# Sample attention of a decoder trunk step: logits and index scores on four column groups, values of four heads in one product per page

## What is computed

```python
NB, ST, PAST, PAGE = 8, 8, 256, 128       # samples, their new tokens, past positions, page
N_KV, GROUP, HEAD_DIM, N_IDX_HEADS, D_IDX = 2, 4, 64, 4, 64
# scores that choose the positions, for each query token of sample b
dots  = einsum('bqhd,bsd->bqhs', qi, ki_all_of_sample_b)
score = einsum('bqh,bqhs->bqs', wi, relu(dots));   top 66 of the 264 positions
# attention over the chosen positions
logits = einsum('bqngd,bqknd->bqngk', q, ks) * 64**-0.5 + bias
p = softmax(logits);   o = einsum('bqngk,bqknd->bqngd', p, vs)
# then, over all 576 tokens, for three branches A (convolution), C (gating), B (attention)
merged = sig(gA)*(yA @ w_pa) + sig(gB)*(yB @ w_pb) + sig(gC)*(yC @ w_pc)
x = LN(alpha*x + (1+g1)*(merged @ w_o));  then a mixture of 16 experts, top 2 inside one group
```

## Time and profile before

| | |
|---|---|
| median of 3 runs (lowest, highest) | 1200.29 us (1197.52, 1201.43) |
| the profiled execution: its own time, its span in the trace | 1202.89 us, 1200.9 us |
| TensorE matmul busy, weight loads busy | 1047.5 us (87%), 715.6 us (60%) |
| VectorE, ScalarE, GpSimd busy | 473.7 us, 181.4 us, 256.0 us |
| mean granted TensorE clock | 0.925 of full speed |
| DMA | 218.4 MB, mean 182 GB/s |

### The profile page before, as it was taken

The page is one execution under the profiler, slowest core; times in us unless marked ns, Lnnn a source line. Parts: engine busy times, 40 slices in busy tenths (PEclk is TensorE's granted clock), DMA queues, the critical chain, the costliest instruction groups (busy, mean ns, idle before and its releaser), DMA issues. The chain is left out here.

```text
span 1200.9 us, 21915 instructions
## 1 busy us (share of the span) xinstructions
PE 1047.5 (87%) x8902; PEld 715.6 (60%) x8902; DVE 473.7 (39%) x1174; ACT 181.4 (15%) x445; POOL 256.0 (21%) x306
## 2 busy tenths in 40 slices
PE   4699999965999989999999999972999999998940
PEld 3577777533776757777877774552655555554520
DVE  0211999912357888662110302446213211110108
ACT  2200112112221211210111110010111111111102
POOL 1300016375221222222223541000100000000034
PEclk9798999987999999998889999995699999999975
DMA  9923536264615223131017207124296999999954
GB/s 318 306 44 114 145 141 232 88 246 164 209 27 154 58 71 128 36 99 34 10 59 170 106 1 291 70 68 193 72 375 255 406 385 381 384 398 415 360 134 128
DMA packets 93570, 218.40 MB, mean 182 GB/s; under 512 B 23696, under 2 KB 42503, under 8 KB 89373
## 3 DMA queue, kind: packets, MB, share of 16 engines
q1 hardware_dynamic: 71428, 183.83, 42.4%
q0 software_dynamic: 5936, 19.16, 5.1%
q10 hardware_dynamic: 16113, 14.06, 3.9%
HBM read 198.95 MB, written 21.06 MB: 183 GB/s over the span
## 5 line engine op out<-in xcount | busy, mean ns | idle before, releaser
L1604 PE MATMUL bank<-arena 128*128 128x288 f32 (+7 forms) x2288 | 609.4, 424 | 33.2 <-DVEq L1259 14.6
L1604 PEld LDWEIGHTS bank<-arena 128*128 128x128 f32 (+2 forms) x2288 | 430.0, 199 | 196.6 <-issue 100.6
L1926 PE MATMUL bank<-arena 128*32 128x256 f32 x3136 | 182.6, 384 | 11.1 <-issue 8.3
L1926 PEld LDWEIGHTS bank<-arena 128*32 128x32 f32 x3136 | 103.1, 110 | 82.5 <-issue 16.3
L1559 DVE TENSOR_TENSOR arena<-arena,bank 128x128 f32<-128x128 f32 x49 | 14.2, 289 | 245.5 <-ACT arena L1070 245.5
L799 POOL TENSOR_SCALAR arena<-arena 128x288 f32<-128x288 f32 x48 | 45.0, 938 | 234.6 <-ACT arena L1036 234.6
L1947 PE MATMUL bank<-arena 128*32 128x256 f32 x1568 | 94.6, 381 | 0.0
L1608 PE MATMUL bank<-arena 128*128 128x128 f32 (+6 forms) x327 | 50.1, 287 | 41.4 <-DVE arena L1371 14.4
L1141 DVE SCALAR_TENSOR_TENSOR arena<-arena 128x512 f32<-128x512 f32 x120 | 81.9, 742 | 0.0
L1608 PEld LDWEIGHTS bank<-arena 128*128 128x128 f32 (+6 forms) x327 | 37.9, 153 | 57.9 <-issue 21.5
L850 POOL DMA_INDIRECT arena<-h,ints x13 | 13.3, 1025 | 267.9 <-PE bank L1908 225.0
(11 more groups left out here) (254 smaller groups left out, 788.7 us busy)
## 6 DMA issues: line engine op xcount, KB each, us to landing
arena<-in_w_e_gate SPq DMA_DIRECT2D x16, 2048.0 KB, 11.3
arena<-in_w_e_up SPq DMA_DIRECT2D x16, 2048.0 KB, 16.0
arena<-in_w_e_down SPq DMA_DIRECT2D x16, 2048.0 KB, 10.8
arena<-in_w_ada SPq DMA_DIRECT2D x12, 2048.0 KB, 12.7
arena<-in_w_in SPq DMA_DIRECT2D x10, 2048.0 KB, 9.9
expert_rows<-arena POOLq DMA_DIRECT2D x1, 5120.0 KB, 17.3
arena<-in_x_prompt SPq DMA_DIRECT2D x8, 512.0 KB, 5.4
expert_rows<-arena ACTq DMA_DIRECT2D x28, 96.0 KB, 7.2
```

Of the source, the lines that this page charges most:

```text
L1604: last = pe.matmul(out, a, b, start=k == 0, stop=k == len(pairs_) - 1)
L1926: last = pe.matmul(out, HG[:, g % 2, k, a:a + BLK], gate_up[i % 2][:, :, k, c * P:c * P + P], start=k == 0, stop=k == KT - 1)
```

## The change

Four things, with the steps of the plan otherwise in their order:

1. The dots and logits of the samples run on four column groups of TensorE. Group g writes 32 of the 128 output partitions: those of key-value group n = g // 2 and of samples 4z to 4z + 3 with z = g % 2. The queries stand in four zeroed copies; copy x holds sample x and sample 4 + x only. So a step has 4 rounds (x) of 4 matmuls (g) of 32 x 256, each accumulating over x, and 4 matmuls of 32 x 64. In the logits the groups 0 and 1 read SBUF partitions 0 to 63 and the groups 2 and 3 read 64 to 127; in the dots all four read the same 64.
2. All copies (`QIM` and `QM`, six of them) are made once, at `("kit", 0)`; the copies at the logits steps and the zeroing at `("kts", 0)` are gone.
3. The values steps of c = 0, 1, 2 are gone; one step `("pv", "s")` stands where that of c = 3 stood. It has one product of 512 columns for the new positions and 16 products, one for each page, with 64 moving columns: 8 tokens x 2 x 4 heads.
4. The transposed probabilities of all four c are kept in `PS4`, which lies where the key pages were. VectorE's copy at `("pt", "s", c)` no longer waits for a values step. The copies of the result have 256 columns, and `yb_up` reaches 17 in place of 20.

```diff
-        if c < NC - 1:
-            sides[at + 2] += [("pv", "s", c)]
...
-            plan += [("gate", "B", f, h)] + ([("pv", "s", NC - 1)] if (f, h) == (0, 0) else []) + [("proj", "B", f, h)]
+            plan += [("gate", "B", f, h)] + ([("pv", "s")] if (f, h) == (0, 0) else []) + [("proj", "B", f, h)]
...
+    QIM, QM = V(A_QM, 2, 4, NS), V(A_QM + 512, NC, 4, NS)
+    PS4 = V(A_KP, NC, 3, P)
...
+    def by_copy(at):
+
+        v = arena[:, at:at + 4 * NS]
+        return bass.AP(v.tensor, v.offset, [list(v.ap[0]), [NS // 2, 2], [NS + ST, 4], [1, ST]])
...
+                own.done(pool.memset(QIM, 0.0))
+                own.link(pool.memset(QM, 0.0))
+                split = lambda q: q.rearrange("p (z r t) -> p z r t", z=2, t=ST)
                 for j in range(2):
...
+                    last = pool.tensor_copy(by_copy(A_QM + j * 4 * NS), split(QIT[:, j, SEQ:NTOK]))
+                    last.then_inc(ev("qim_ready"), 1)
+                for c in range(NC):
+                    last = pool.tensor_copy(by_copy(A_QM + 512 + c * 4 * NS), split(QT[:, c, SEQ:NTOK]))
+                    last.then_inc(ev("qm_ready"), 1)
-            elif key == ("kts", 0):
...
-            elif kind == "lg" and key[1] == "s":
...
-                    q, qn = QMN[c % 2]
                     pe.wait_ge(ev("qm_ready"), c + 1)
...
-                    group(ps[:, 0:PAST], [(q[:, b, :], KTS[:, b, :]) for b in range(NB)])
-                    last = pe.matmul(ps[:, PAST:PAST + NS], qn, KTT[:, SEQ:NTOK], start=True, stop=True)
+                    head = lambda g: slice((g // 2) * HD, (g // 2) * HD + HD)
+                    for x in range(4):
+                        for g in range(4):
+                            z = g % 2
+                            pe.matmul(ps[32 * g:32 * g + 32, 0:PAST], QM[head(g), c, x, 32 * z:32 * z + 32], KTS[head(g), 4 * z + x, :], start=x == 0, stop=x == 3)
+                    for g in range(4):
+                        q = SEQ + 32 * (g % 2)
+                        last = pe.matmul(ps[32 * g:32 * g + 32, PAST:PAST + NS], QT[head(g), c, q:q + 32], KTT[head(g), SEQ:NTOK], start=True, stop=True)
...
-                    pe.wait_ge(*tt.taken(("pt", i, c)))
-                    pe.matmul(ps[:, 0:P], VA[0:NS, 4, :], PTT[0:NS, 0, 256:384], start=True, stop=False)
-                    out4 = ps[:, 0:P].rearrange("p (n b t) -> p n b t", n=NKV, b=NB)
+                    for c2 in range(NC):
+                        pe.wait_ge(*tt.taken(("pt", "s", c2)))
+                    pe.matmul(ps.rearrange("p (c x) -> p c x", c=NC), VA[0:NS, 4, :], PS4[0:NS, :, 2, :], start=True, stop=False)
+                    out5 = ps.rearrange("p (c n b t) -> p c n b t", c=NC, n=NKV, b=NB)
                     for b in range(NB):
                         for k in range(NPG):
-                            pt4 = PTT[:, 0, k * P:k * P + P].rearrange("p (n b t) -> p n b t", n=NKV, b=NB)
-                            last = pe.matmul(out4[:, :, b, :], VP[:, NPG * b + k, :], pt4[:, :, b, :], start=False, stop=(b, k) == (NB - 1, NPG - 1))
+                            p5 = PS4[:, :, k, :].rearrange("p c (n b t) -> p c n b t", n=NKV, b=NB)
+                            last = pe.matmul(out5[:, :, :, b, :], VP[:, NPG * b + k, :], p5[:, :, :, b, :], start=False, stop=(b, k) == (NB - 1, NPG - 1))
```

65 lines of the change are left out of this document (23 added, 42 removed).

## The result

| | before | after |
|---|---|---|
| median (lowest, highest) | 1200.86 us (1197.52, 1202.91), 4 runs | 1167.64 us (1163.97, 1169.45), 4 runs |
| ratio | | 0.9724, 95% interval 0.9702 to 0.9745 |
| profiled execution: own time, span | 1202.89, 1200.9 us | 1167.23, 1165.3 us |
| mean granted TensorE clock | 0.925 | 0.928 |

The change makes the kernel 2.8% faster. The forecast was 1163.3 us, with a range of 1158.5 to 1172. The medians differ by 33.2 us, the two profiled executions by 35.7. A later set of five runs of the changed kernel had a median of 1164.49 us.

The account below looks back on a forecast made before the run. TensorE was taken to bound the samples' attention. Gains 6.9 + 15.2 + 2.4 + 13.7 less 0.4, 0.45 and 0.4 make 37.0 us, from the median 1200.3 to 1163.3 us, range 1158.5 to 1172.

Parts of the forecast that it names:

- Dots, 6.9: Samples' dots on TensorE: four steps fall from 3.72 to 2.0 us each, a gain of 6.9 us.
- Logits, 15.2: Samples' four logits steps: 23.2 us falls to 8.0, a gain of 15.2 us, 8.7 of it regained clock.
- Wait for the copies, 2.4: TensorE's idle time before the first logits step, ahead of GpSimd's copies, goes: a gain of 2.4 us, counted once.
- Values, 13.7: Three values steps go, a gain of 13.7 us; the last one grows, a loss of 0.45 plus 0.4 us.
- the bound of 1.4 us more: Last values step: upper bound on extra time for its 16 page products if loads and moving columns add up.
- What is late next, 0.4: After the first logits step TensorE waits for VectorE's probabilities: a loss of 0.4 us, bounds 0 and 1.
- Not counted: Behind the last values step: up to 1.7 us more gained if 64 moving columns keep the clock up.
- Row halves that take turns: Rival, chance 0.13: a logits step's two row halves do not run together, 3.8 us a step, 1170 us in all.
- The Trainium skill's 62 ns: Dots and logits: sequencer time per matmul with hardware decode off; eight steps would together cost an estimated 4 us more.
- The clock did not fall on narrow products: Rival, chance 0.07: narrow dots and logits products let the clock fall, costing 13 us, 1176 us in all.
- VectorE did not take the gain of the dots: Rival, chance 0.06: in the dots units VectorE takes at most the 6.9 us gain, 1170 us in all.
- Four column groups on 64 rows do overlap: Rival, chance 0.04, claimed no overlap in dots and logits: 7.6 us a step, 45 us more, 1208 us in all.

## Why the prediction was right, point by point

The sum was 37.0 us, the middle gave 36.5.

- **Dots, 6.9.** Taken at 2.0 us a step, measured 1.98: 4 x (3.72 - 1.98) = 7.0. From the first dots to the first logits 6.8 us less were spent; 0.2 went to slightly longer rows between the steps. The experts' row as the nearest one was the right choice: from 484.76 to the next row at 486.52 it is 1.76 us for 32 records, 55 ns each.
- **Logits, 15.2.** 5.39 + 5.24 + 5.94 + 6.62 = 23.2 us before, 4 x 1.98 = 7.9 now: 15.3. The size was right, the reason half of it. I said that the clock comes back because the values steps that stood ahead are gone. With the values steps gone and the copies late, the four wide logits still took 22.6 us; with the copies in time as well, 14.4. So the clock hung on both, and of the 15.3 us 14.4 - 7.9 = 6.5 are the narrow shape and 23.2 - 14.4 = 8.8 the clock (8.7 was said). For the first logits step the prediction named the pause of 2.40 us ahead, but gave no reason why that should cost clock, and left 2.0 us in its range for it; with the pause gone the wide step takes 3.73 us in place of 5.39, so the pause it was.
- **Wait for the copies, 2.4.** Gained, as said. But the reason that the text gave for counting it once, that the later logits steps had their copies in time, was true only while values steps stood there. With late copies the changed kernel loses 9.1 us. The sum came out right because the early copies went in together with the rest.
- **Values, 13.7.** Gone. The last step: 1.06 us for the first product in place of 0.42, 1.12 in place of 0.72 for the copies, 5.96 in place of 4.88 in all: a loss of 1.08 where 0.85 was said. The 512-column product was mis-sized by 0.2 us; it costs the upper bound of 1.1. The page products cost the same with 64 columns as with 16, 3.79 and 3.75 us, so the loads set the pace, and the bound of 1.4 us more was not touched.
- **What is late next, 0.4.** The wait for the probabilities is 0.29 us. One round in the logits made it 1.58, so this was a real wall close behind.
- **Not counted: up to 1.7 for the clock behind the last values step.** It came in nine of eleven executions with 64 columns at this step, and was lost again to a slow stretch later in eight of the nine. Leaving it out was right for a reason that I did not have.

By these terms: 6.8 + 15.3 + 2.4 + 13.7 - 0.3 - 1.1 = 36.8, less 0.4 for the pairs and transposes between the logits steps, which take 12.17 us in place of 12.12 and once 0.2 more: 36.4 from the first dots to branch B. Behind it the 1.7 us at branch B came and went.

**The rivals.** Row halves that take turns would have shown a logits step of 3.8 us beside a dots step of 2.0. Both are 1.98. By this row two row halves that write different quadrants of one bank run together. The Trainium skill quotes that different row tiles cannot (PSUM — Partial Sum Buffer, PSUM bank collisions raise a hardware error); this measurement decides against it for different quadrants. The Trainium skill's 62 ns (TensorE: Matmul & The Clock Gate, Wait — 56ns, not 53.3ns?) are for one matmul with hardware decode off. The prediction held them against 56 ns a record, but a float32 matmul has two records, so the experts' rows have 112 ns a matmul and say nothing against it. Only the double dots steps are below it: 64 records, 32 matmuls, were issued from 491.54 to the next row at 493.27, 54 ns a matmul. Which decode setting was on, no run shows. The clock did not fall on narrow products: 1.00 in all windows. VectorE did not take the gain of the dots. Four column groups on 64 rows do overlap: 1.98 us, not 7.6.

**The total.** 1163.3 was said, and 1167.64 and 1164.49 came in two sets. The miss of 4.3 us is not in the middle, which is 0.5 us from its sum. It lies in the spread of the same kernel: its executions reach from 1162.34 to 1170.55 us. In the profiled ones the stretch ahead of the middle is 483.7 and 479.6 us, with the code of that part unchanged, while the stretch behind it is 350.3 and 351.3. The range of 1158.5 to 1172 allowed for it.

## What to carry to other kernels

Price a step by the row of the nearest shape that runs in the same way, here another part of the kernel on four column groups, and look at the granted clock before you call a duration a cost of the instruction: 8.8 of the logits' 23.2 us belonged to what stood ahead of them, products with 16 moving columns or a pause. Before you count a removed wait once, ask of each other place whether it was hidden by something that the change removes too. And compare kernels between two marks that both have: the middle repeated within 0.1 us in two profiled executions of the changed kernel whose whole times were 3.2 us apart. Count the slow stretches between the marks first, since one more or less is 1.7 us.

## What the runs showed that I had not expected

- Weight loads of 128 columns under 16-column products run at 118 ns a record at full clock and at 209 ns at half, and TensorE that is never idle still loses its clock on them.
- A column group can start a later product before an earlier one of another group: six 64-column records before three 256-column ones that precede them in the program.
- Eight tiles of 64 x 32 at once, two row halves by four column groups into two banks: 64 records of 256 columns in 1.97 us, the time that 32 take (1.94).
- Slow stretches of 1.7 us seem to change places rather than to go: none later in the five executions slow at branch B's start, eleven in the nine that were not.
- The clock can fall in a pause of TensorE itself: 0.50 before the first product behind pauses of 2.39 and 3.46 us, but 1.00 all through three others of 2.59 us.
- GpSimd's small copies, made a step too late, cost more than their waits: 12.8 us of waits and 8.2 of clock in the wide products behind the pauses.
